# A two-block transformer kernel: the first modulation and projection by halves of the features, and four modulation slabs moved into layer 0's routing

## The reference

```python
for l in range(DEPTH):                              # DEPTH = 2
    mod   = silu(c)     @ w_ada[l] + b_ada[l]       # (1024) @ (1024, 6144)
    mod_c = silu(c_ctx) @ w_ada[l] + b_ada[l]
    sh1, sc1, g1, sh2, sc2, g2 = split(mod, 6)      # 1024 each; the same for ctx
    h  = rms_norm(x,  norm1_g[l]) * (1 + sc1)  + sh1
    hc = rms_norm(xc, norm1_g[l]) * (1 + csc1) + csh1
    y, yc = mixer(h, hc)        # h @ w_in[l] (1024, 4608): 1536 for Fourier and attention, 3072 gates
    x = x + g1 * y
    h = rms_norm(x, norm2_g[l]) * (1 + sc2) + sh2
    x = x + g2 * experts(h)     # 16 experts, each takes its 32 best tokens of the 256, SwiGLU
    # layer 0 does the same for the context tokens
```

## Time and profile before

| what | value |
|---|---|
| median of three runs | 2400.65 us |
| profiled execution, its own time | 2398.58 us |
| its span, first to last instruction | 2396.8 us |
| PE busy | 2006.8 us (84% of the span) |
| PE weight loads busy | 1101.1 us (46%) |
| DVE busy, ACT busy | 624.1 us (26%), 437.5 us (18%) |
| moved by DMA | 576.33 MB, 240 GB/s over the span |
| mean granted PE clock | 0.955 of full |

### The profile page before, as it was taken

The page is one execution under the profiler, slowest core; times in us unless marked ns, Lnnn a source line. Parts: engine busy times, 40 slices in busy tenths (PEclk is TensorE's granted clock), DMA queues, the critical chain, the costliest instruction groups (busy, mean ns, idle before and its releaser), DMA issues.

```text
span 2396.8 us, 31615 instructions
## 1 busy us (share of the span) xinstructions
PE 2006.8 (84%) x13634; PEld 1101.1 (46%) x13634; DVE 624.1 (26%) x1481; ACT 437.5 (18%) x1103; POOL 21.9 (1%) x42
## 2 busy tenths in 40 slices
PE   6997999997988888889999865567766599989997
PEld 4444554445333333334768531223332247654765
DVE  2012450035111212213351410201101235322542
ACT  2112531112111101002151110100000122222222
POOL 2000000000000000000000000000000000000000
PEclk8999999998999999999999888888989899999999
DMA  9444215611999999994313379999999922232320
GB/s 340 150 174 148 99 56 191 210 71 71 379 409 409 408 409 409 404 408 183 138 39 139 138 310 409 409 403 406 403 403 406 358 106 106 75 137 105 106 79 18
DMA packets 191208, 576.33 MB, mean 240 GB/s; under 512 B 7424, under 2 KB 16080, under 8 KB 191072
## 3 DMA queue, kind: packets, MB, share of 16 engines
q1 hardware_dynamic: 188096, 567.31, 61.7%
q0 software_dynamic: 2512, 6.84, 0.9%
q10 hardware_dynamic: 464, 0.16, 0.0%
HBM read 573.24 MB, written 1.05 MB: 240 GB/s over the span
## 4 chain that ended last, share of the span: by engine, by line
PE 49%; DMA 24%; issue 8%; PEld 7%; DVE 5%; ACT 3%; PEldq 3%; SPq 1%; DVEq 0%
DMA ring<-w_up_e 15%; PE ps L731 7%; PE ps L720 6%; PE ps L1144 5%; DMA ring<-w_down_e 4%; PE ps L899 4%; PE ps L1057 3%; PEld ps L1088 3%; PE ps L1152 3%; DMA ring<-w_xkv 3%; PEldq L685 3%; PE ps L747 2%; PE ps L1285 2%; PEld ps L949 1%; PE ps L1120 1%
## 5 line engine op out<-in xcount | busy, mean ns | idle before, releaser
L1057 PE MATMUL ps<-ring,reg_bc 128*32 128x512 f32 x3072 | 396.2, 652 | 177.3 <-DMA ring<-w_up_e 169.7
L1057 PEld LDWEIGHTS ps<-ring,reg_bc 128*32 128x32 f32 x3072 | 94.2, 115 | 459.7 <-DMA ring<-w_up_e 271.1
L731 PE MATMUL ps<-reg_a,ring 128*128 128x512 f32 (+1 forms) x768 | 256.3, 490 | 7.3 <-issue 4.4
L731 PEld LDWEIGHTS ps<-reg_a,ring 128*128 128x128 f32 x768 | 144.1, 191 | 106.3 <-issue 92.2
L2184 DVE TENSOR_TENSOR xall<-xall,ps 128x512 f32<-128x512 f32 x48 | 32.8, 687 | 472.4 <-PE ps L1029 472.4
L1144 PE MATMUL ps<-ring,reg_a 128*128 128x512 f32 (+2 forms) x448 | 147.9, 486 | 7.9 <-issue 6.0
L720 PE MATMUL ps<-ring,reg_a 128*128 128x512 f32 (+1 forms) x352 | 141.1, 555 | 1.8 <-issue 1.5
L1634 ACT ACTIVATE reg_bc<-ps 128x512 f32<-128x512 f32 x48 | 28.7, 597 | 616.0 <-PE ps L1057 616.0
L2227 DVE TENSOR_TENSOR reg_a<-ps,reg_e 32x256 f32<-32x256 f32 x192 | 80.7, 420 | 202.3 <-PE ps L1088 199.9
L1088 PE MATMUL ps<-ring,reg_bc 128*32 128x256 f32 x2048 | 117.5, 380 | 16.4 <-issue 12.1
L1144 PEld LDWEIGHTS ps<-ring,reg_a 128*128 128x128 f32 x448 | 76.0, 195 | 74.0 <-issue 70.9
(11 more groups left out here) (334 smaller groups left out, 2106.8 us busy)
## 6 DMA issues: line engine op xcount, KB each, us to landing
ring<-w_gate_e SPq DMA_DIRECT2D x128, 1024.0 KB, 12.2
ring<-w_up_e SPq DMA_DIRECT2D x128, 1024.0 KB, 15.6
ring<-w_down_e SPq DMA_DIRECT2D x64, 2048.0 KB, 16.2
ring<-w_in SPq DMA_DIRECT2D x34, 2048.0 KB, 8.2
ring<-w_ada SPq DMA_DIRECT2D x24, 2048.0 KB, 8.1
ring<-w_out SPq DMA_DIRECT2D x8, 2048.0 KB, 8.9
ring<-w_xkv SPq DMA_DIRECT2D x8, 1024.0 KB, 16.2
ring<-w_br_global SPq DMA_DIRECT2D x4, 1024.0 KB, 6.4
```

The source lines that it names most:

```text
L731: mm = pe.matmul(ps[j][:, 0:n], w[:, k, j * P:(j + 1) * P], HT[:, k, 0:n], start=(k == 0), stop=(k == KC - 1))
L1057: mm = pe.matmul(ps[s][32 * j:32 * j + 32, :], XGT[:, s, 2 * q + k, e * CAP:(e + 1) * CAP], w[:, j // 2, k, (j % 2) * COL:(j % 2 + 1) * CO ...
```

## The change

1. **Opening by halves.** The plan begins `ada 0, ada 2, qkv 0, ada 1, ada 3` in place of `ada 0 to 3, qkv 0`. Slabs 0 and 2 are the shift and the scale of features 0 to 511. All four tiles' chunks 0 to 5 are turned by chunk into six banks (`first_turn`), and chunks 0 to 3 are modulated over all tokens, two instructions of 128x256 a chunk. Then the first `qkv` slab is multiplied in parts (`first_part`): contraction chunks 0 to 3 of each tile first, with slabs 1 and 3 of `w_ada` between them, and chunks 4 to 7 after. The row and column steps of these four slabs stay on DVE. Three releases come together at the end of the first `qkv` slab. POOL waits for the third product in place of three used slabs.
2. **Sixteen products in the mixer, not twenty.** None stands beside `qkv 1` and `branch 1` any more; the others move up by two.
3. **Four products in layer 0's routing** (numbers 20 to 23, `ADA_LAST = 20`). They use bank 2 for product and turning; each waits for the column step of the one before. `scaled_rows`, which writes that bank too, waits for all. In the plan they stand after the two `out` slabs, ahead of the experts.
4. **Routing order.** On PE tile 1 is turned ahead of tile 0's logits, into banks 6 and 7, and `turn_slots(1)` stands behind `turn_affinities(0)`. On DVE tile 0's modulation and tile 1's normalisation and modulation stand ahead of the threshold. `modulation(1, 1)` goes from the mixer's end to behind the selections.

PE in the opening, before: `L652` is a product of one slab, `L640` its turning, `L706` the tiles' turning, `L720` the first `qkv` slab.

The diff, cut to what the text speaks of:

```diff
@@ -41,7 +41,8 @@
 MIX = 1536
 DIN2 = 4096
 LN2PI = 6.283185307179586
-ADA_FIRST = 4
+ADA_FIRST = (0, 2, 1, 3)
+ADA_LAST = 20
 MEMORY_FROM = 6
 MEMORY_TURNED = 5
 
@@ -49,15 +50,20 @@
 def slab_plan():
 
     plan = []
-    plan += [("ada", 0, s) for s in range(ADA_FIRST)]
     for l in range(DEPTH):
         mixer = [("qkv", s) for s in range(3)] + [("gate", s) for s in range(3)] + [("branch", 0)]
         mixer += [("gate", 3 + s) for s in range(3)] + [("branch", 1)]
         for n, (kind, s) in enumerate(mixer):
-            if l == 0 and n:
-                plan += [("ada",) + divmod(ada, 12) for ada in (2 + 2 * n, 3 + 2 * n)]
+            if l == 0 and n == 0:
+                plan += [("ada", 0, ADA_FIRST[0]), ("ada", 0, ADA_FIRST[1]), (kind, l, s),
+                         ("ada", 0, ADA_FIRST[2]), ("ada", 0, ADA_FIRST[3])]
+                continue
+            if l == 0 and 2 <= n < 10:
+                plan += [("ada",) + divmod(ada, 12) for ada in (2 * n, 2 * n + 1)]
             plan.append((kind, l, s))
         plan += [("out", l, s) for s in range(2)]
+        if l == 0:
+            plan += [("ada",) + divmod(ada, 12) for ada in range(ADA_LAST, 24)]
         for e in range(E):
             plan += [("expert", l, 6 * e + s) for s in range(4)]
             if l and 0 <= e - MEMORY_FROM < 8:
...
-        gp.wait_ge(slab_used, ADA_FIRST - 1)
+        gp.wait_ge(*at("ada_mm@0", 3))
...
-        def ada_product(n):
+        def ada_product(n, b=6, held=False):
...
-            pe.wait_ge(*(at(f"ada_row@{l}", s) if s else at("ada_row@0", 12)))
+            if n == 0:
+                pe.wait_ge(*at("ct", 1))
+            elif n >= ADA_LAST:
+                pe.wait_ge(*at(f"ada_done@{l}", s))
+            else:
+                pe.wait_ge(*(at(f"ada_row@{l}", m) if m else at("ada_row@0", 12)))
...
+            if not held:
+                last_release(pe)
...
+        def first_turn(k, t):
+
+            pe.wait_ge(*at("n1@0_xn", t + 1))
+            b = k if k < 6 else k - 2
+            mm = pe.transpose(ps[b][:, t * P:t * P + P], XN[:, t, k * P:k * P + P], ident[:, :])
+            if t == 3:
+                mm.then_inc(sem(f"n1@0_t{k % 2}"), 1)
+
+        def first_part(t, k0, k1):
+
+            i = where[("qkv", 0, 0)]
+            w = slab_view(i)
+            slab_wait(pe, i)
+            for k in range(k0, k1):
+                pe.wait_ge(*at(f"n1@0_ht{k % 2}", k // 2 + 1))
+                mm = pe.matmul(ps[t][:, :], HT[:, k, t * P:t * P + P], w[:, k, :], start=(k == 0), stop=(k == KC - 1))
+            if k1 == KC:
+                group_done(mm, "qkv@0", t)
...
@@ -789,27 +802,51 @@
         def mixer(l):
             tokens = 4 * P if l == 0 else 2 * P
             if l == 0:
-                n1_turn(0, 0)
-            n1_turn(l, 1)
-            qkv_group(l, 0, 0)
-            n1_turn(l, 2)
-            qkv_group(l, 0, 1)
-            n1_turn(l, 3)
-            if l == 0:
-                qkv_group(l, 0, 2)
-                qkv_group(l, 0, 3)
-            last_release(pe)
+                ada_product(0)
+                ada_turn(0)
+                ada_product(2)
+                for t in range(4):
+                    for k in range(6):
+                        first_turn(k, t)
+                ada_turn(2)
+                first_part(0, 0, 4)
+                first_part(1, 0, 4)
+                ada_product(1, held=True)
+                first_part(2, 0, 4)
+                ada_turn(1)
+                ada_product(3, held=True)
+                first_part(3, 0, 2)
+                ada_turn(3)
+                first_part(3, 2, 4)
+                first_part(0, 4, 6)
+                for k in (6, 7):
+                    for t in range(4):
+                        first_turn(k, t)
+                for t in range(1, 4):
+                    first_part(t, 4, 6)
+                for t in range(4):
+                    first_part(t, 6, 8)
+                for slab in range(3):
+                    last_release(pe)
+            else:
+                n1_turn(l, 1)
+                qkv_group(l, 0, 0)
+                n1_turn(l, 2)
+                qkv_group(l, 0, 1)
+                n1_turn(l, 3)
+                last_release(pe)
             for s in (1, 2):
                 for t in range(4):
                     qkv_group(l, s, t)
                     if l == 0:
-                        ada = 2 + 2 * s + t // 2
                         step = 2 * (s - 1) + t // 2
                         if t % 2 == 0:
-                            ada_product(ada)
+                            if s == 2:
+                                ada_product(4 + t // 2)
                             fourier_tokens(0, step)
                         else:
-                            ada_turn(ada)
+                            if s == 2:
+                                ada_turn(4 + t // 2)
                             fourier_channels(0, step)
...
             for j in range(4):
                 branch_groups(l, 1, j, tokens)
-                if l == 0 and j % 2 == 0:
-                    ada_product(22 + j // 2)
-                elif l == 0:
-                    ada_turn(22 + j // 2)
...
+                pe.wait_ge(*(at("ada_done@1", ADA_LAST - 12) if l == 0 else at("ada_done@1", 12)))
...
             turn_tile(0)
-            logits(0)
-            turn_tile(1)
-            logits(1)
             if l == 0:
+                pe.wait_ge(*at("rexp@0", 1))
+                ada_product(ADA_LAST, 2)
+                turn_tile(1)
+                ada_turn(ADA_LAST, 2)
+                logits(0)
+                logits(1)
+                ada_product(ADA_LAST + 1, 2)
+                turn_affinities(0)
+                ada_turn(ADA_LAST + 1, 2)
                 turn_slots(1)
-            turn_affinities(0)
-            if l == 0:
+                ada_product(ADA_LAST + 2, 2)
                 gather(0, 1, 0)
+                ada_turn(ADA_LAST + 2, 2)
                 gather(0, 1, 1)
+                ada_product(ADA_LAST + 3, 2)
+                ada_turn(ADA_LAST + 3, 2)
+                pe.wait_ge(*at("ada_done@1", 12))
...
+        def first_mod(k):
+            act.wait_ge(*at("n1@0_t0", k // 2 + 1))
+            for s in range(2):
+                ins = act.activation(HT[:, k, s * SEQ:(s + 1) * SEQ], ps[min(k, 4)][:, s * SEQ:(s + 1) * SEQ], ACT.Identity,
+                                     scale=SCL[:, 0, 0, k, s:s + 1], bias=MODT[:, 0, k, s:s + 1])
+            ins.then_inc(sem("n1@0_ht0"), 1)
...
+                for half in range(2):
+                    act.wait_ge(*at("mod@0", half + 1))
+                    first_mod(4 * half)
+                    first_mod(4 * half + 2)
...
+            if l == 0:
+                ada_row(ADA_LAST, 2)
             modulated_tile(1)
+            if l == 0:
+                ada_column(ADA_LAST, 2)
             exps(0)
+            if l == 0:
+                ada_row(ADA_LAST + 1, 2)
             act.preload_act_table(ACT.Sigmoid)
             if l == 0:
+                ada_column(ADA_LAST + 1, 2)
+                ada_row(ADA_LAST + 2, 2)
                 rows_in(0, 1, 0)
+                ada_column(ADA_LAST + 2, 2)
                 rows_in(0, 1, 1)
+                ada_row(ADA_LAST + 3, 2)
+                ada_column(ADA_LAST + 3, 2)
...
             if l == 0:
-                for t in range(4):
-                    n1_normed(0, t)
-                ada(0, 0, ADA_FIRST)
-                modulation(0, 0)
-                n1_mod(0, 0)
-                n1_mod(0, 1)
-                n1_mod(0, 2)
+                n1_normed(0, 0)
+                ada_row(0)
+                n1_normed(0, 1)
+                ada_column(0)
+                n1_normed(0, 2)
+                n1_normed(0, 3)
+                ada_row(1)
+                ada_column(1)
+                first_modulation(0)
+                first_mod(1)
+                first_mod(3)
+                ada_row(2)
+                ada_column(2)
+                ada_row(3)
+                ada_column(3)
+                first_modulation(1)
+                first_mod(5)
+                first_mod(7)
                 qkv_in(0, 0, 1)
-                n1_mod(0, 3)
                 qkv_in(0, 0, 3)
...
-                modulation(1, 1)
...
                 normed(0)
                 eight(1, 2)
                 add_out_group(1, 1)
+                modulated_tile(0)
+                normed(1)
                 eight(1, 3)
+                modulated_tile(1)
                 threshold()
-                normed(1)
-                modulated_tile(0)
-                modulated_tile(1)
                 slots(1)
                 softmax(0)
...
                 select(s, 4, E, f"sel@{l}")
+            if l == 0:
+                modulation(1, 1)
```

171 lines of the change are left out of this document (78 added, 93 removed).

## The result

The changed kernel takes 2386.58 us, the median of seven runs (2375.27 to 2390.86), beside 2399.97 for the kernel before (seven runs, 2393.43 to 2402.11): ratio 0.994, interval 0.9919 to 0.996. The forecast was 2387.5. Two later groups of runs of the same changed kernel gave 2384.29 and 2384.38, the second without one slow run of 2430.21. The profiled execution is the longest of the seven, 2390.86 with a span of 2389.1 us, so its stages are read with the two further traces beside them (experiments 8 and 11).

What follows compares the result with a forecast made beforehand. PE was taken to bound mixer and opening, the weight stream the experts; -7.6 opening, -9.4 mixer, +4.2 routing gave -12.8, from 2398.58 to 2385.8; the median standing 2.1 higher, 2387.5 was forecast, range 2381.5 to 2397.

Steps and rivals of the forecast that it cites:

- first part of `qkv 0` starts: Opening: the first part of the first `qkv` slab starts at 28.7 us, or 31.0 with turnings at half clock.
- opening: First `qkv` stage: PE works without a gap and ends at 62.6 instead of 70.2 us, a gain of 7.6.
- `qkv 1`: Mixer: two product-and-turning pairs fewer at 2.2 us a pair, all on PE's path, a gain of 4.5 us.
- `branch 1`: Mixer: two product-and-turning pairs fewer at 2.5 us a pair, all on PE's path, a gain of 4.9 us.
- routing: Layer 0's routing with four products: grows by 4.2 us, bounds 1.9 to 8.8, logits and product 21 partly at half clock.
- experts: Expert stage: keeps its length, with the ring full when the DMA engines start the next transfer.
- the rival in which it gives half: Mixer: DVE's merges set the pace in `branch 1`, only `qkv 1` pays; -7.9 in all, 2392.7 us, chance 0.05.
- the rival with its first 4.1 us at half clock: Opening: turnings and first parts at half clock, gain only 3.4; -8.6 in all, 2392 us, chance 0.15.
- PE cold through the routing: Layer 0's routing at half clock: it grows by 8.8; -8.2 in all, 2392.5 us, chance 0.14.
- Held by `scaled_rows` and not by DVE: Routing: `turn_slots(0)` comes 33 us after `turn_tile(0)`, with PE's `scaled_rows` and not DVE's chain setting the end.
- whether the fifth slab lands in time: Opening: the last slab lands at 37.4, no later than 40.4; PE asks for it at 41.6 us, so it is hidden.
- The rival on the other side: Expert stage: the four slabs delay the experts' weight stream, adding 20.5 us; +7.7 in all, 2408 us, chance 0.04.

Runs made afterwards that it cites:

- experiment 8: The changed kernel run again, same instructions, with a second trace: 2384.29 us, ratio 0.995 to the kernel before.
- experiment 11: The changed kernel run a third time, same instructions, with another trace: 2384.38 us, ratio 0.9933 to the kernel before.
- experiment 9: Repeat of the changed kernel with all four routing products moved into PE's gaps: 2378.27 us, ratio 0.9913 to the kernel before.
- experiment 2: Changed kernel with the old opening put back, the rest as changed: 2397.06 us, ratio 0.9992 to the kernel before.
- experiment 4: Changed kernel with `turn_slots(1)` and `turn_affinities(0)` ahead of product 21 on PE: 2383.73 us, ratio 0.9935 to the kernel before.
- experiment 5: Changed kernel with products 20 and 21 behind tile 0's turning, 22 behind the logits, 23 between the gathers: 2379.28 us, ratio 0.9924 to the kernel before.
- experiment 10: Changed kernel with product 21 directly behind 20, `turn_affinities(0)` and `turn_slots(1)` right after the logits: 2380.63 us, ratio 0.9924 to the kernel before.
- Experiment 1: Kernel before with only the opening by halves; all twenty later products in the mixer, routing as before: 2407.4 us, ratio 1.0031.
- experiment 3: Changed kernel with the routing's four slabs only loaded and released, no products (computes something else): 2378.8 us, ratio 0.9914 to the kernel before.

## Why the prediction was right

The sum was -12.8, and 2387.5 stood against 2386.58 measured. The terms, by the prediction's own steps:

| term | forecast | kernel after | |
|---|---|---|---|
| first part of `qkv 0` starts | 28.7 | 28.07 | 26.78 to 29.48 in other traces with this opening |
| opening | -7.6 | -9.0 | by the stage's end, 61.2 instead of 70.2 |
| `qkv 1` | -4.5 | -5.2 | `qkv 1` to `qkv 2`: 38.38 before, 33.12 after |
| `branch 1` | -4.9 | -5.1 | output stage starts 19.3 us earlier |
| output stage | 0 | +1.7 | +1.7 in all three traces; half clock at and behind tiles 2 and 3's logits |
| routing | +4.2 | +8.1 | +2.7 and +5.5 in the other two traces |
| experts | 0 | 0 | 501.46 us after, 501.63 before |

The opening was read rightly down to its mechanism: the slabs had landed, the tiles had been normalised, and PE had only been waiting for four modulation slabs in a row. It came out 1.4 us better than said: the first part started 0.6 earlier, and the two products took 1.95 each and not 2.24, since the next part follows them at once. The fifth slab and POOL's later loads cost nothing. The mixer's two stages gave 10.3 us, so the rival in which it gives half is out.

**The clock in the opening.** The 16 records of the first part take 7.1 us in every trace with this opening, so the rival with its first 4.1 us at half clock did not occur. The prediction read the rise at 41 us in the kernel before as following turnings, and missed an earlier one in the same trace, behind the second product (20.07 to 23.3):

```profile
22.00:23.00 1.00, 1.00 (x27) 0.86 (x17) 0.94 (x3) 0.00 (x0) 0.00 (x0) 0.50 1.05 387
...
24.00:25.00 1.00, 0.00 (x0) 0.00 (x0) 0.11 (x1) 0.00 (x0) 0.00 (x0) 1.00 0.98 369
```

There PE then waited 2.70 us for the next slab, and the clock was back at 0.50 by 28 us. In the new opening the turnings follow that product at once. In the kernel after, the 24 turnings take 3.56 us against 2.83 in experiment 9, so the full clock came on during them. The Trainium skill, "TensorE: Matmul & The Clock Gate", section "Part 4: PE-mode transpose", says that transposes don't bring it on. The trace does not refute its rule: a product of 2 to 3.6 us always stood ahead of the turnings, and a kernel with turnings alone was not tried. Its consequence here, a gain of 3.4 instead of 7.6, is refuted.

**The routing is the term that was mis-sized.** The step reads "I take 4.2, logits and product 21 partly at half clock". The bounds were 1.9 to 8.8, and three traces of one kernel gave +8.1, +2.7 and +5.5, mean 5.4, as the clock was at half for 20, 7 and 13 us. The prediction took the clock from one trace as a trait of the place. It differs from execution to execution: the kernel before has 16 windows of 1 us at 0.50 there (567 to 583), experiment 2 also 16, experiment 4 ten. The forecast median came out right because 4.2 lies among the sizes that occur and the mixer and opening gave 2.3 us more than said. That it came within 1 us is luck: the output stage, for which the sum had no term, took 1.7 of it back (it takes 68.2 us in the three traces, 66.6 before and 64.9 in experiment 5, where its clock stays at 1.00), and with the mean of the three traces for the routing the terms add up to -12.2, with the first trace's +8.1 to -9.5. The first trace's routing is close to that of the rival "PE cold through the routing" (+8.8, chance 0.14), and all three traces had between 7 and 20 us at half clock. The same stage carries part of the scatter of the runs, 2375 to 2391. Another part lies where nothing was changed: from layer 1's first projection to the span's end the traces of the changed kernel take 1299.2, 1294.4 and 1297.2 us, and the one of before 1297.2. Why was not looked into.

**What was named as holding the stage.** "Held by `scaled_rows` and not by DVE" holds: `scaled_rows` (L1003) waits for product 23's column, 0.81 us, and `turn_slots(0)` for ACT behind it, while DVE's chain had ended 7.7 us earlier. The stage's length was forecast at 33 us and came out at 37.2, 31.8 and 34.6. Product 20 filled half of the old gap of 5.45 us, 2.24 stayed. In all five traces with this wait the clock falls at its end or within 3.2 us of it; in the three without it (experiments 5, 9 and 10) it doesn't fall there. That the gap is the cause is not shown. In experiments 4 and 8 the clock falls only 2.7 and 3.1 us behind it, while the logits with their 16 moving columns run, and the 2.10 us gap of experiments 5 and 9 did not bring it down. What is shown is that the order of experiment 5 kept the clock up in both of its traces, and that of the change in none of three.

**What the prediction did not see** is that the parts are no sum. It counted -7.6 for the opening and -4.5 for `qkv 1` as two terms. Experiment 1 has the first without the second (and without the other two parts) and is 0.31% slower than before (7.4 us by the ratio, 9.3 by the medians). The reason could be read beforehand: three slabs held to the stage's end against the ring's look-ahead and the order in the plan. The prediction asked only whether the fifth slab lands in time, not when the next one can be asked for.

**The rival on the other side**, four slabs in the experts' stream, did not occur: the experts' first wait is for ACT, their stage has the old length, and in experiment 3 the same four loads without products gave 2378.8.

## What to carry to other kernels

When a stage holds buffers of a ring to its end, look at the request of the slab after them and not only at the landing of those within: a head start can be spent whole on the next wait. Small matrix work moved into a stage with gaps should go first into the gaps in which PE would wait for another engine, here behind tile 0's turning, behind the logits and between the gathers; it then cost nothing (27.2 us against 28.0 without the products and with sixteen windows at half clock), and the clock stayed up in both traces, while in other places of the routing the same work cost 3.8 to 9.2 us. A stage that runs at half clock in one trace should be bounded from both clocks, and traced more than once before its size is believed.
